# The first 64 key tiles as wide products with the halves added on VectorE, and lookups summed in one operation

## What is computed

```python
s = jnp.einsum('thpd,hpnd->thpn', q, sub_keys)            # 8 heads, 2 halves, 128 sub-keys
top_s, top_i = lax.top_k(s, PEER_TOPK)                    # 16 of 128, for each half
cand = top_s[:, :, 0, :, None] + top_s[:, :, 1, None, :]
best_s, best_c = lax.top_k(cand.reshape(..., 256), PEER_TOPK)
i1 = jnp.take_along_axis(top_i[:, :, 0], best_c // PEER_TOPK, axis=-1)
i2 = jnp.take_along_axis(top_i[:, :, 1], best_c % PEER_TOPK, axis=-1)
gate = jax.nn.softmax(best_s, axis=-1)
h = jnp.einsum('thkd,td->thk', u_tab[i1 * 128 + i2], xc)
act = jax.nn.gelu(h, approximate=False) * gate
y = jnp.einsum('thk,thkd->td', act, v_tab[i1 * 128 + i2])
```

## Time and profile before

| | us |
|---|---|
| median of three runs | 1035.49 (1034.63 to 1035.78) |
| the profiled execution | 1034.91 |
| its span, first to last instruction | 1033.1 |
| TensorE busy | 1022.0 (99%) |
| VectorE busy | 811.6 (79%) |
| ScalarE busy | 523.5 (51%) |
| GpSimd busy | 543.1 (53%) |

### The profile page before, as it was taken

One profiled execution on the slowest core, in us unless ns is written; L12 is line 12 of the kernel. 1 busy time (PEld: TensorE's weight loads), 2 busy tenths in 40 slices (PEclk: granted clock), 3 DMA queues, 4 the chain that ended last, 5 costly groups with the idle time before them and its releaser, 6 DMA issues.

```text
span 1033.1 us, 21169 instructions
## 1 busy us (share of the span) xinstructions
PE 1022.0 (99%) x7326; PEld 912.7 (88%) x7326; DVE 811.6 (79%) x1348; ACT 523.5 (51%) x851; POOL 543.1 (53%) x230
## 2 busy tenths in 40 slices
PE   9999989999999999999999999999999999999998
PEld 9998979999999999998888888777777778888886
DVE  6999684667899999456666666899999997677664
ACT  5653857544544444545555555544444445454543
POOL 4654454564689999873334333533444334444442
PEclk9999999999999999999999999999999999999999
DMA  6684434554455555554555455555555555655662
GB/s 236 228 285 134 139 104 146 207 197 152 136 192 182 176 188 178 173 193 148 178 172 173 163 172 175 179 168 180 163 163 178 170 179 184 195 191 186 200 193 91
DMA packets 52330, 181.93 MB, mean 176 GB/s; under 512 B 5911, under 2 KB 9123, under 8 KB 52164
## 3 DMA queue, kind: packets, MB, share of 16 engines
q1 hardware_dynamic: 52148, 181.42, 54.0%
q10 hardware_dynamic: 144, 0.00, 0.0%
HBM read 180.33 MB, written 3.43 MB: 178 GB/s over the span
## 4 chain that ended last, share of the span: by engine, by line
PE 95%; DVE 3%; ACT 1%; issue 1%; POOL 1%; ACTq 0%; DVEq 0%; POOLq 0%
PE bank L1219 34%; PE bank L1534 33%; PE bank L1475 12%; PE bank L1477 6%; PE bank L1489 3%; PE bank L1319 2%; DVE prob L854 1%; PE bank L1234 1%; PE bank L1451 1%; DVE nrm L1143 1%; PE bank L1243 1%; PE bank L1335 0%; POOL lo L344 0%; PE bank L1358 0%; ACT hi L327 0%
## 5 line engine op out<-in xcount | busy, mean ns | idle before, releaser
L344 POOL TENSOR_TENSOR lo<-raw,hi 128x1024 fp32r<-128x1024 f32 x216 | 540.2, 2510 | 475.2 <-ACT hi L327 474.8
L327 ACT CAST hi<-raw 128x1024 fp32r<-128x1024 f32 x332 | 347.5, 1048 | 223.6 <-PE bank L1534 190.9
L1219 PE MATMUL bank<-nrm,hi 128*128 128x256 f32 x1600 | 291.6, 285 | 0.1
L1534 PE MATMUL bank<-hi,nrm 128*128 128x512 f32 x1024 | 285.2, 395 | 1.4 <-DVE nrm L1143 1.4
L1219 PEld LDWEIGHTS bank<-nrm,hi 128*128 128x128 f32 x1600 | 250.4, 193 | 2.2 <-issue 1.6
L1534 PEld LDWEIGHTS bank<-hi,nrm 128*128 128x128 f32 x1024 | 187.3, 188 | 45.7 <-DVE nrm L1143 10.1
L1219 PE MATMUL bank<-nrm,lo 128*128 128x256 f32 x800 | 227.0, 284 | 0.0
L1143 DVE TENSOR_TENSOR nrm<-act,nrm 128x256 fp32r<-128x256 f32 x128 | 180.8, 1414 | 50.0 <-ACT nrm L659 50.0
L344 DVE TENSOR_TENSOR lo<-raw,hi 128x1024 fp32r<-128x1024 f32 x116 | 149.0, 1285 | 44.6 <-ACT hi L327 44.4
L1475 PE MATMUL bank<-nrm,hi 128*128 128x512 f32 x512 | 181.8, 399 | 0.0
L1534 PE MATMUL bank<-lo,nrm 128*128 128x512 f32 x512 | 158.2, 390 | 0.0
(11 more groups left out here) (186 smaller groups left out, 976.9 us busy)
## 6 DMA issues: line engine op xcount, KB each, us to landing
raw<-u_tiles SPq DMA_DIRECT2D x128, 512.0 KB, 3.3
raw<-v_tiles SPq DMA_DIRECT2D x128, 512.0 KB, 3.4
raw<-front SPq DMA_DIRECT2D x76, 512.0 KB, 3.6
toeplitz<-bias_row SPq DMA_DIRECT2D x6, 384.0 KB, 7.7
bias<-toeplitz SPq DMA_DIRECT2D x12, 128.0 KB, 3.5
resid<-x_t SPq DMA_DIRECT2D x2, 512.0 KB, 4.7
qk<-sub_keys SPq DMA_DIRECT2D x1, 1024.0 KB, 7.9
y<-act SPq DMA_DIRECT2D x2, 512.0 KB, 2.6
```

Of the source, the lines that this page charges most:

```text
L327: act_e.copy(hi[:, s, :], raw[:, s, :]).then_inc(hi_ready, 1)
L344: eng.tensor_tensor(lo[:, s, :], raw[:, s, :], hi[:, s, :].bitcast(F32), ALU.subtract)\
L1219: ins = pe.matmul(dst, w_[:, s, u * P:(u + 1) * P], x_[:, k, :], start=first and i == 0 and p_ == 0, stop=last and i == n - 1 and p_ == 2)
L1534: ins = pe.matmul(bank[2 * c + half][:, :], a_[:, j, c * P:(c + 1) * P], v_[:, j, half * 512:(half + 1) * 512], start=False, stop=stop and ...
```

## The change

The first 64 key tiles go through `wide_tile` as well. For tiles 0 to 55 it uses a ring of four banks (4 to 7), and a tile waits for the addition of the tile four before it; from tile 56 on it uses banks 4 and 5 as before, and from tile 58 on a tile waits for the addition two before it. In the first half ScalarE copies the right half into one of four slices `first_sum` instead of `half_sum`, and takes the gelu of the tile two before. VectorE adds the halves at the end of each of its 64 turns in the loop over tiles, behind the routing steps of that tile; the loop is followed by the copy of the transposed choices, as before. The routing steps are placed over tiles 0 to 51, by other weights. The Exp stands before tile 56 on ScalarE, and the softmax at tile 58 on VectorE. The transposes stay after tile 59. In a lookup one reduction over the innermost of (head, k, j) replaces the four halving additions.

```diff
-TOP_TILES = 48
-EXP_TILE = 52
-PICK_TILE = 60
+TOP_TILES = 52
+WIDE_RING = 56
...
+        first_sum = part(86, 4).rearrange("p (a t) -> p a t", a=RING)
...
+        def sums(first, j):
+            return first_sum[:, j % RING, :] if first else half_sum[:, j % 2, :]
...
-            def gelu(base_i, it, j):
+            def copy_cross(base_i, it, j, b):
 
                 a.wait_ge(pe_step, it * 4 + (S_U + base_i + j + 1))
-                a.activation(act[:, it * 4 + (base_i + j), :], bank[4 + j % 2][:, 0:T], ACT.Gelu).then_inc(gelu_done, 1)
...
-            a.preload_act_table(ACT.Gelu)
...
+                buffers = RING if base_i < HALF else 2
+                if not (isinstance(it, int) and it == 0 and j < buffers):
+                    a.wait_ge(gelu_done, it * 4 + (base_i + j + 1 - buffers))
+                a.copy(sums(base_i < HALF, j), bank[b][:, T:2 * T]).then_inc(crossed, 1)
+            def gelu_sum(base_i, it, j, first=False):
+                a.wait_ge(added, it * 4 + (base_i + j + 1))
+                a.activation(act[:, it * 4 + (base_i + j), :], sums(first, base_i + j), ACT.Gelu).then_inc(gelu_done, 1)
+            def first_keys(it, ring, first=False):
                 for j in range(RING):
                     split_hi(a, U0 + LEAD, it, j)
-                    gelu(0, it, j)
+                    copy_cross(0, it, j, 4 + j % ring)
+                    if not (first and j < 2):
+                        gelu_sum(-2, it, j, True)
+            a.preload_act_table(ACT.Gelu)
+            first_keys(0, RING, first=True)
+            with a.Fori(1, WIDE_RING // RING) as it:
+                first_keys(it, RING)
 
...
-            with a.Fori(EXP_TILE // RING, HALF // RING) as it:
-                for j in range(RING):
-                    split_hi(a, U0 + LEAD, it, j)
-                    gelu(0, it, j)
+            with a.Fori(WIDE_RING // RING, HALF // RING) as it:
+                first_keys(it, 2)
+            for j in range(2):
+                gelu_sum(HALF - 2, 0, j, True)
 
             a.wait_ge(pick_ready, 2)
...
-                    copy_cross(it, j)
+                    copy_cross(HALF, it, j, 4 + j % 2)
                     if not (first and j == 0):
-                        gelu_sum(-1, it, j)
+                        gelu_sum(HALF - 1, it, j)
...
-                    src_, to = eq, eq_sum
-                    for level in range(4):
-                        n = TOPK * TOPK >> level + 1
-                        pair = src_[:, 0:2 * n * PH].rearrange("p (h a n) -> p h a n", h=PH, a=2)
-                        out_ = sel[:, w, c, :] if level == 3 else to[:, 0:n * PH]
-                        link(dve.tensor_tensor(out_.rearrange("p (h n) -> p h n", h=PH), pair[:, :, 0], pair[:, :, 1],
-                                               ALU.add))
-                        src_, to = to, src_
+                    link(dve.tensor_reduce(sel[:, w, c, :].rearrange("p (h k) -> p h k", h=PH),
+                                           eq[:, :].rearrange("p (h j k) -> p h k j", h=PH, k=TOPK), AX.X, ALU.add))
...
-            weights = [21] * HALVES + [13] + TC * ([23] + [35] * (PH // 2) + [8] + [13, 13, 18] * 2 + [3])
+            def add_halves(base_i, it, j, b):
+                dve.wait_ge(crossed, it * 4 + (base_i + j + 1))
+                both = sums(base_i < HALF, j)
+                dve.tensor_tensor(both, bank[b][:, 0:T], both, ALU.add).then_inc(added, 1)
+            weights = [21] * HALVES + [25] + TC * ([13] + [35] * (PH // 2) + [25] + [13, 18, 12] * 2 + [3])
             tile_of = [int(TOP_TILES * sum(weights[:n]) / sum(weights)) for n in range(len(weights))]
...
-                if i == EXP_TILE + 2:
+                if i == WIDE_RING + 2:
                     softmax_gates()
+                add_halves(0, 0, i, 4 + i % (RING if i < WIDE_RING else 2))
             dve.wait_ge(pick_T, 1)
...
-            for job in JOBS[-4:]:
-                if BANK_OF[job] < 6:
-                    freed(pe, job)
-
-            def u_tile(base_i, it, j):
-
-                wait(pe, gelu_done, it * 4 + (base_i + j - 1))
-                ins = product(bank[4 + j % 2][:, 0:T], j, [(k, k) for k in range(KB)], nrm_hi, nrm_lo, U0 + base_i, it, j)
-                ins.then_inc(pe_step, 1)
-
-            def wide_tile(it, j, last=False):
-
-                b = bank[4 + j % 2]
-                if isinstance(it, int) and it == 0 and j < 2:
-                    pe.wait_ge(gelu_done, HALF + j - 1)
+            def wide_tile(base_i, it, j, ring, last=False):
+                b = bank[4 + j % ring]
+                if isinstance(it, int) and base_i + 4 * it + j < RING:
+                    freed(pe, [job for job in JOBS[-RING:] if BANK_OF[job] == 4 + j][0])
+                elif ring == RING or isinstance(it, int) and base_i + 4 * it + j < WIDE_RING + 2:
+                    pe.wait_ge(added, it * 4 + (base_i + j - 3))
                 else:
-                    pe.wait_ge(added, it * 4 + (j - 1))
-                wait_lo(pe, U0 + HALF, it, j)
+                    pe.wait_ge(added, it * 4 + (base_i + j - 1))
+                wait_lo(pe, U0 + base_i, it, j)
                 for k in range(KB):
                     unit = slice(k * P, (k + 1) * P)
                     pe.matmul(b[:, :], hi[:, j, unit], nrm[:, k, :, :].rearrange("p a t -> p (a t)"),
...
+            def first_keys(it, ring):
+                for j in range(RING):
+                    wide_tile(0, it, j, ring)
             pe.wait_ge(nlo, 2 * KB)
-            for j in range(RING):
-                u_tile(0, 0, j)
-            with pe.Fori(1, PICK_TILE // RING) as it:
-                for j in range(RING):
-                    u_tile(0, it, j)
-
-            freed(pe, ("sc", N_SC - 1))
+            first_keys(0, RING)
+            with pe.Fori(1, WIDE_RING // RING) as it:
+                first_keys(it, RING)
+            first_keys(WIDE_RING // RING, 2)
...
-            with pe.Fori(PICK_TILE // RING, HALF // RING) as it:
-                for j in range(RING):
-                    u_tile(0, it, j)
+            with pe.Fori(WIDE_RING // RING + 1, HALF // RING) as it:
+                first_keys(it, 2)
```

More of the change, by code:

```diff
@@ L238, in hybrid_block @@
         eq = part(96, 4).bitcast(F16)
-        eq_sum = part(100, 2).bitcast(F16)
         place = part(102, 1).bitcast(F16)[:, 0:TOPK * TOPK].rearrange("p (j k) -> p j k", k=TOPK)
@@ L622, in _ @@
                     "p (u n) -> p u n", n=NK)).then_inc(act_evac, 1)
-            def gelu(base_i, it, j):
+            def copy_cross(base_i, it, j, b):
                 a.wait_ge(pe_step, it * 4 + (S_U + base_i + j + 1))
-                a.activation(act[:, it * 4 + (base_i + j), :], bank[4 + j % 2][:, 0:T], ACT.Gelu).then_inc(gelu_done, 1)
-            a.preload_act_table(ACT.Gelu)
-            with a.Fori(0, EXP_TILE // RING) as it:
+                buffers = RING if base_i < HALF else 2
[6 more added lines that the diff above has]
+            def first_keys(it, ring, first=False):
                 for j in range(RING):
                     split_hi(a, U0 + LEAD, it, j)
-                    gelu(0, it, j)
+                    copy_cross(0, it, j, 4 + j % ring)
[5 more added lines that the diff above has]
+                first_keys(it, RING)
             a.wait_ge(top_done, 1)
@@ L637, in _ @@
             a.preload_act_table(ACT.Gelu)
-            with a.Fori(EXP_TILE // RING, HALF // RING) as it:
-                for j in range(RING):
-                    split_hi(a, U0 + LEAD, it, j)
-                    gelu(0, it, j)
+            with a.Fori(WIDE_RING // RING, HALF // RING) as it:
+                first_keys(it, 2)
+            for j in range(2):
+                gelu_sum(HALF - 2, 0, j, True)
             a.wait_ge(pick_ready, 2)
-            def copy_cross(it, j):
-                a.wait_ge(pe_step, it * 4 + (S_U + HALF + j + 1))
-                a.wait_ge(gelu_done, it * 4 + (HALF + j - 1))
-                a.copy(half_sum[:, j % 2, :], bank[4 + j % 2][:, T:2 * T]).then_inc(crossed, 1)
-            def gelu_sum(base, it, j):
-                a.wait_ge(added, it * 4 + (base + j + 1))
-                a.activation(act[:, it * 4 + (HALF + base + j), :], half_sum[:, (base + j) % 2, :], ACT.Gelu)\
-                 .then_inc(gelu_done, 1)
             def a_split(base_i, it, j):
@@ L675, in _ @@
             key_round(HALF // RING - 1, last=True)
-            gelu_sum(HALF - 1, 0, 0)
+            gelu_sum(N_U - 1, 0, 0)
             a.wait_ge(pe_step, S_V)
@@ L1144, in low_part @@
                                   ALU.subtract).then_inc(a_lo, 1)
-            def add_halves(it, j):
-                dve.wait_ge(crossed, it * 4 + (j + 1))
-                dve.tensor_tensor(half_sum[:, j % 2, :], bank[4 + j % 2][:, 0:T], half_sum[:, j % 2, :], ALU.add)\
-                   .then_inc(added, 1)
             def gate_body(half, it, first=False, last=False):
@@ L1169, in gate_body @@
                             low_part(0, 0, 0)
```

(4 more changed lines are left out.)

## The result

| | before | after |
|---|---|---|
| median, us | 1034.89 (1034.37 to 1035.78, six runs) | 1040.63 (1040.13 to 1042.12, six runs) |
| span of the profiled execution | 1033.1 | 1038.7 |
| granted clock, mean | 0.998 | 0.996 |

What follows compares the result with a forecast made beforehand. TensorE, busy for 99% of the span, was taken as the bound; -6.6 + 0.3 + 4.6 + 1.4 = -0.3 us gave a forecast of 1035.2 us, no measurable change, with a range from 1032.8 to 1039.6 us.

Steps and rivals of the forecast that it cites:

- VectorE's lateness: Tiles 32 to 51: additions lag tiles by up to 7.8 us, under the 8.2 us allowed, so cost nothing.
- the lookup's sum: One reduction replacing four halving additions in each of four lookups: 2.33 us each, bounds 1.22 and 2.74 us.
- both groups: Routing steps in tiles 32 to 37 and 45 to 51, where the additions' lag peaks: 7.8 and 7.1 us.
- margins: Room left under the 8.2 us lag: 0.4 us in tiles 32 to 37, 1.1 us in tiles 45 to 51.
- the candidates and the last steps: Routing steps on VectorE in the lag sums of tiles 32 to 51: 2.33 us and 0.33 us each.
- The first rival: VectorE becomes the bound in tiles 33 to 53, giving 1039.0 us; chance 0.27.
- The rate: TensorE in tiles 0 to 63: 2.777 us a tile instead of 2.881, a gain of 6.6 us.
- The low bound of 0: Least gain from TensorE's rate, if something in the first half held the wide tile at the old rate.
- the rival: The rate isn't gained: first half's wide tile stays at 2.88 us, giving 1041.8 us; chance 0.03.
- The boundary: After tile 63, before the gate products: TensorE idles 4.6 us for VectorE's uncovered sequence; ends 4.2 and 8.8 us.
- the clock behind it: After the idle time before the gate products: TensorE's clock falls to 0.50, costing 1.4 us.
- the Exp: ScalarE's Exp, moved from tile 52 to 56, delays the start of tile 58: +0.3 us.

Runs made afterwards that it cites:

- e1: Kernel after with the lookup's reduction over neighbouring fp16 elements, which sums the wrong axis: 1038.35 us, ratio 1.0033.
- e6: Kernel after with one small fp16 matmul of 64 columns before tile 0: 1039.22 us, ratio 1.0045.
- e7: Kernel after with one small fp16 matmul of 64 columns before every fourth of the first 64 tiles: 1041.30 us, ratio 1.0064.
- e10: e11 with the one small fp16 matmul of e6 before tile 0 added: 1028.46 us, ratio 0.9940 to the kernel before.
- e13: Kernel after with one small fp32 matmul before tile 0: 1040.99 us, ratio 1.0061.
- e14: Kernel after with tile 0 waiting for ScalarE's copy of the last scores, no extra matmul: 1040.23 us, ratio 1.0061.
- e2: Kernel after with each four-bank tile from tile 4 on also waiting for the copy of the tile two before: 1041.33 us, ratio 1.0061.
- e3: Kernel after with VectorE's work on the choices moved behind addition 59 and two one-hot groups behind additions 60 and 61: 1039.64 us, ratio 1.0042.
- e5: Kernel after with the four halving additions put back in each lookup in place of the reduction: 1047.14 us, ratio 1.0125.
- e9: Kernel after with the buffer laid out so that the right axis is innermost for the reduction: 1038.78 us, ratio 1.0035.
- e11: e12 with the layout of e9 and routing weights by the measured lengths: 1031.08 us, ratio 0.9966 to the kernel before.
- e12: Kernel after with transposes, Exp and softmax earlier, choices taken from PSUM, one one-hot operation behind each of additions 58 to 63: 1034.29 us, ratio 0.9996.
- e4: Kernel before with a wait for the previous tile's gelu in the middle of each narrow tile: 1035.52 us, ratio 1.0010.
- e8: Kernel before with one small fp16 matmul before every fourth of its first 64 tiles: 1037.00 us, ratio 1.0020.

## Why the prediction was wrong

**VectorE's lateness, costed at nothing; the lookup's sum in it.** "I take 2.33 us with its wait, the nearest in kind", with 2.74 us as the upper bound. Both came from rows over neighbouring elements. The diff shows `(h j k) -> p h k j`, which reads with a stride of 32 bytes, and I took no account of it. It measured 4.32 us. The bound was none, as it was taken from another access pattern. With 4.32 us the prediction's own sums would have put both groups about 4.0 us later and 3.6 + 2.9 us over their margins. Measured were 2.9 us. By chance other steps were shorter, as they met GpSimd less: in the first group the product took 2.06 us where I had 3.36, and in the last one a comparison and product took 1.23 us each (423.25 and 424.85 above), 2.5 us for the pair where I had 4.61. The sum is not all of it, either. e1 has sums of 2.28 us, as I took them, and TensorE waited for 1.2 us before tiles 41 and 55 all the same; I had charged the candidates and the last steps at their undisturbed lengths. So "I cost it at nothing" failed, for 1.8 of 3.0 us by the sum and for the rest by such steps. The first rival, VectorE as the bound, was right in kind, at the place named (tiles 33 to 53); steps held up by GpSimd were its reason, the strided sum was not.

**The rate.** "14 pairs, 0.347 us a pair" was read in the second half and carried over. "I see nothing that would" hold the tile at another rate: the wide form has two paces, 0.3467 and 0.3533 us, and the first half started in the slower one. That is 2.9 of 6.6 us. The low bound of 0 covered it, but the rival had been made all or nothing. Why the first half started in the slower pace stays open.

**What was right.** The boundary (4.6 against 4.5 us) and its uncovered place, the clock behind it (1.4 against 1.6 us, with 0.50 granted), and the Exp (0.3 against 0.2 us). The windows of the kernel after behind the gate products (window, length, busy by engine, clock, DMA):

```profile
464.00:465.00 1.00, 0.86 (x17) 0.86 (x17) 0.96 (x3) 0.00 (x0) 0.00 (x0) 0.50 0.02 4
...
467.00:468.00 1.00, 1.00 (x8) 0.88 (x7) 0.00 (x0) 0.00 (x0) 0.00 (x0) 1.00 0.00 0
```

Two misses of 2.9 us, both in the same direction, make the difference between "no change" and a loss of 0.56%, and put it 1 us over the range's upper end.

**What stays open.** What about the start of a stream of wide matmuls sets its pace. In the profiled executions a changed start set the faster one in all five kernels that have it (e6, e7, e10, e13, e14), and all eight with tile 0 as it was started in the slower one (the kernel after, e1, e2, e3, e5, e9, e11, e12). But the same small matmul before tile 8 of e7 was followed by the slower pace, and a stall threw the pace either way (to the slower in e6, to the faster in e1 and e3). No run took a stall of one given length alone. Open, too, is what decides whether the clock falls behind a wait of 3 us (it did in e3 and not in e5).

## What to carry to other kernels

Bound an operation by a row with its access pattern, not only its count: the innermost stride of the read doubled this one. Before a step is moved ahead of a deadline, ask what each of its pieces costs beside GpSimd: pieces of 2.3 us were free one at a time between deadlines 2.7 us apart (e10), and cost 3.4 us of waits in a row (e3). A change that loses may hold a gain that its order hides: the same wide products, with that order, the near layout and the new weights, gained 3.7 us (e11), and 6.4 us with one small matmul in front (e10).

## What the runs showed of the hardware

- A reduction over 2048 fp16 elements a partition: 2.28 us over neighbours, 4.32 us over elements 32 bytes apart (e1 and e9 against the kernel after).
- A pair of a 512-column and a 256-column fp32r matmul has two steady paces at the full granted clock, 0.3467 and 0.3533 us, which last until the next interruption. Three matmuls of 256 columns took 0.360 us in the first half, in e4 and e8 too.
- The lower of TensorE's clocks followed a wait of its weight loads of 4.6 us and also one of 3.0 us (e3), but not one of 3.1 us (e5).
- VectorE operations on two operands in SBUF took 0.42 to 0.60 us with GpSimd idle and 2.1 to 2.8 us beside its splits (the kernel after against e3).
